# Stick-breaking attention: outputs of two heads side by side, logits of a head in both row halves, fewer abs passes on ScalarE

## The reference, cut to what matters

```python
z = jnp.einsum("bhqd,bhkd->bhqk", qi, kj).astype(jnp.float32)
valid = jnp.logical_or(jnp.logical_not(is_diag), diag_mask)
lo = jnp.where(valid, jax.nn.log_sigmoid(-z), 0.0)
after = jnp.einsum("bhqj,js->bhqs", lo, later) + acc[..., None]
logw = jnp.where(valid, z + lo + after, -jnp.inf)
o = o + jnp.einsum("bhqk,bhkd->bhqd", jnp.exp(logw).astype(vj.dtype), vj).astype(jnp.float32)
acc = acc + jnp.sum(lo, axis=-1)
```

## Time and profile before

| | us |
|---|---|
| median of 3 runs | 2718.43 |
| lowest and highest | 2717.89, 2723.14 |
| the profiled execution's own time | 2719.01 |
| its span, first to last instruction | 2717.3 |
| TensorE busy in it | 2547.8 (94%) |
| GpSimd busy | 1498.4 (55%) |
| VectorE busy | 1039.9 (38%) |
| ScalarE busy | 558.3 (21%) |

### The profile page before, as it was taken

One profiled execution on the slowest core, in us unless ns is written; L12 is line 12 of the kernel. 1 busy time (PEld: TensorE's weight loads), 2 busy tenths in 40 slices (PEclk: granted clock), 3 DMA queues, 4 the chain that ended last, 5 costly groups with the idle time before them and its releaser, 6 DMA issues.

```text
span 2717.3 us, 34707 instructions
## 1 busy us (share of the span) xinstructions
PE 2547.8 (94%) x14410; PEld 2061.8 (76%) x14410; DVE 1039.9 (38%) x1667; ACT 558.3 (21%) x1127; POOL 1498.4 (55%) x1396
## 2 busy tenths in 40 slices
PE   7998997999999998999999989868589998999998
PEld 6778886888888886568888878645488687888887
DVE  3443857163051401336404164973542151421023
ACT  1112323021020113741102021224332210210010
POOL 7444554587496664337749636621121565666664
PEclk9997998999999998999999998989798999999999
DMA  5222022233232231003324313210000222333321
GB/s 165 78 56 63 1 86 85 78 115 95 70 123 94 80 107 62 1 32 105 98 69 124 93 45 90 64 53 16 1 3 2 74 86 85 93 98 97 93 79 69
DMA packets 104289, 199.06 MB, mean 73 GB/s; under 512 B 9306, under 2 KB 12612, under 8 KB 104132
## 3 DMA queue, kind: packets, MB, share of 16 engines
q1 hardware_dynamic: 101476, 189.36, 22.8%
q10 hardware_dynamic: 2656, 7.47, 0.8%
HBM read 194.71 MB, written 2.10 MB: 72 GB/s over the span
## 4 chain that ended last, share of the span: by engine, by line
PE 84%; DVE 10%; ACT 2%; POOL 2%; issue 1%; SPq 0%; DMA 0%; DVEq 0%; POOLq 0%; ACTq 0%
PE psum L153 34%; PE psum L293 23%; PE psum L155 7%; PE psum L232 3%; PE psum L1260 1%; PE psum L1251 1%; PE psum L1279 1%; POOL weight_split_ring L412 1%; DVE big L1810 1%; PE psum L2090 1%; PE psum L2099 1%; DVE best L1809 1%; PE psum L968 1%; PE psum L2075 1%; PE psum L194 1%
## 5 line engine op out<-in xcount | busy, mean ns | idle before, releaser
L412 POOL TENSOR_TENSOR weight_split_ring<-weight_ring,weight_split_ring 128x512 fp32r<-128x512 f32 (+2 forms) x732 | 955.6, 1326 | 30.6
L153 PE MATMUL psum<-x_split,weight_split_ring 128*128 128x512 f32 x4080 | 963.1, 396 | 1.9 <-POOL weight_split_ring L412 1.3
L153 PEld LDWEIGHTS psum<-x_split,weight_split_ring 128*128 128x128 f32 x4080 | 770.2, 190 | 173.3 <-issue 11.8
L409 POOL TENSOR_SCALAR weight_split_ring<-weight_ring 128x1024 fp32r<-128x1024 f32 (+2 forms) x366 | 395.6, 1081 | 759.0 <-PE psum L293 339.9
L293 PE MATMUL psum<-weight_split_ring,hidden_split 128*128 128x512 f32 x2448 | 576.5, 396 | 8.2 <-DVEq L2899 8.2
L293 PEld LDWEIGHTS psum<-weight_split_ring,hidden_split 128*128 128x128 f32 x2448 | 460.3, 188 | 120.0 <-DVEq L2899 8.6
L155 PE MATMUL psum<-weight_split_ring,x_split 128*128 128x512 f32 (+2 forms) x1056 | 238.0, 385 | 2.0 <-DVEq L2899 1.4
L155 PEld LDWEIGHTS psum<-weight_split_ring,x_split 128*128 128x128 f32 x1056 | 195.2, 205 | 43.7 <-issue 7.2
L708 DVE TENSOR_TENSOR big<-big 128x512 f32<-128x512 f32 x64 | 89.0, 1391 | 178.4 <-ACT big L693 178.4
L511 DVE SCALAR_TENSOR_TENSOR residual<-residual,psum 128x512 f32<-128x512 f32 x48 | 32.8, 682 | 261.9 <-PE psum L293 261.9
L693 ACT ACTIVATE big<-psum 128x512 f32<-128x512 f32 x64 | 38.3, 599 | 434.9 <-PE psum L153 378.8
(11 more groups left out here) (329 smaller groups left out, 2627.6 us busy)
## 6 DMA issues: line engine op xcount, KB each, us to landing
weight_ring<-in_mlp_w SPq DMA_DIRECT2D x128, 512.0 KB, 3.8
weight_ring<-in_w_in SPq DMA_DIRECT2D x92, 512.0 KB, 3.6
weight_ring<-in_w_ffn_in SPq DMA_DIRECT2D x40, 512.0 KB, 3.6
weight_ring<-in_w_out SPq DMA_DIRECT2D x24, 512.0 KB, 3.7
weight_ring<-in_w_ffn_out SPq DMA_DIRECT2D x22, 512.0 KB, 3.6
weight_ring<-in_sb_w_q SPq DMA_DIRECT2D x8, 512.0 KB, 3.6
weight_ring<-in_sb_w_k SPq DMA_DIRECT2D x8, 512.0 KB, 3.8
weight_ring<-in_sb_w_v SPq DMA_DIRECT2D x8, 512.0 KB, 3.7
```

What stands on the lines that cost most here:

```text
L153: mm = pe.matmul(out, wp[:, k, m * P:(m + 1) * P], xp, start=first, stop=last)
L409: pool.tensor_scalar(part.high[:, 0:nk, 0:n], raw, 1.0, 0.0, ALU.mult, ALU.add).then_inc(self.high_made, 1)
L412: low = pool.tensor_tensor(part.low[:, k, 0:n], raw[:, k, :], part.high[:, k, 0:n].bitcast(F32), ALU.subtract)
```

## The change

- `out` is done for a pair of heads p (2p, 2p+1) in steps with even h: for each block first the product of the even head, into partitions 0 to 63 of PSUM, then that of the odd head, into 64 to 127 of the same bank. It waits for the selects of both heads. `wt` gets a third buffer. ScalarE's copy and VectorE's `low` handle a pair at once, 128 partitions instead of 64.
- From head 2 on, the logits of blocks 1, 2 and 3 read copies of q and k that stand in the other row half (`m.swap`, two buffers, one a pair); block 0 stays in the head's own half. ScalarE issues the two DMA transfers of a pair's copies: pairs 1 and 2 at the start of the stage, pairs 3 to 7 in steps 4, 6, 8, 10 and 12, behind the weights pass. TensorE waits for them before the first block of a head (`s_sw`).
- For the first two spans (768 columns) softplus is made as Ln(1 + Exp(min(z, 40))) and then the maximum with z. The minimum is a new VectorE pass, `clamp(h)`, PSUM to SBUF; ScalarE does Exp on it, without Abs. Block 0 keeps Abs, Exp(-x), Ln. VectorE's order per step becomes clamp(h+1), softplus(h), low; ScalarE's stays ln(h+1), weights of h, copy.

The diff, cut to its core:

```diff
@@ -1197,9 +1197,9 @@
     s_z = kit.sem("sb_logits_ready")
-    s_abs = kit.sem("sb_abs_ready")
-    s_exp = kit.sem("sb_exp_ready")
-    s_ln = kit.sem("sb_ln_ready")
+    s_sw = [kit.sem(f"sb_other_half_landed{n}") for n in range(2)]
+    s_cl = kit.sem("sb_clamped_logits_ready")
+    s_soft = kit.sem("sb_last_abs_then_exp_then_ln_ready")
     s_lo = kit.sem("sb_softplus_ready")
     s_t = kit.sem("sb_later_blocks_summed")
     s_x = kit.sem("sb_exponent_ready")
@@ -1209,6 +1209,7 @@
     s_oh = kit.sem("sb_out_high_ready")
     s_of = kit.sem("sb_out_read")
+    LINEAR = 40.0
     START = [0, 512, 896, 1152]
     BANK = [(0, 0), (1, 0), (2, 0), (2, 256)]
@@ -1240,6 +1241,16 @@
     def rows(h):
         return slice((h % 2) * 64, (h % 2) * 64 + 64)
+
+    def other_q(h, b):
+        return m.swap[rows(h + 1), (h // 2) % 2, 0, (b - 1) * P:]
+
+    def other_k(h, b):
+        return m.swap[rows(h + 1), (h // 2) % 2, 1, (b - 1) * P:b * P]
+
+    def weights(h, b):
+        c = START[b]
+        return m.wt[:, h % 3, c:c + SEQ - b * P]
     def tensor(pe):
         def logits(h):
@@ -1247,9 +1258,14 @@
                 if h >= 2:
                     pe.wait_ge(s_w, NS * (h - 2) + n + 1)
+                    if n == 0:
+                        pe.wait_ge(s_sw[(h // 2) % 2], 32 * ((h // 2 + 1) // 2))
                 for b in blocks:
-                    mm = pe.matmul(bank(h, b), m.kF[rows(h), h // 2, b * P:(b + 1) * P], m.qF[rows(h), h // 2, b * P:],
-                                   start=(b != 3), stop=True, skip_group_check=True)
+                    if h >= 2 and b >= 1:
+                        k, q = other_k(h, b), other_q(h, b)
+                    else:
+                        k, q = m.kF[rows(h), h // 2, b * P:(b + 1) * P], m.qF[rows(h), h // 2, b * P:]
+                    mm = pe.matmul(bank(h, b), k, q, start=(b != 3), stop=True, skip_group_check=True)
                 mm.then_inc(s_z, 1)
         def exponents(h):
@@ -1269,15 +1285,15 @@
                                        start=False, stop=True, skip_group_check=True)
                 mm.then_inc(s_x, 1)
-        def out(h):
-            if h >= 2:
-
-                pe.wait_ge(s_of, h - 1)
-            o = kit.psum[rows(h), 6 + h % 2, :]
-            pe.wait_ge(s_cut, h + 1)
+        def out(p):
+            if p >= 2:
+
+                pe.wait_ge(s_of, p - 1)
+            pe.wait_ge(s_cut, 2 * p + 2)
             for b in range(NT):
-                mm = pe.matmul(o[:, b * P:], m.vTok[:, b, h * 64:(h + 1) * 64], packed(m.wt, h, b),
-                               start=(b == 0), stop=(b == NT - 1), skip_group_check=True)
+                for h in (2 * p, 2 * p + 1):
+                    mm = pe.matmul(kit.psum[rows(h), 6 + p % 2, b * P:], m.vTok[:, b, h * 64:(h + 1) * 64], weights(h, b),
+                                   start=(b == 0), stop=(b == NT - 1), skip_group_check=True)
             mm.then_inc(s_o, 1)
         logits(0)
@@ -1286,53 +1302,77 @@
                 logits(h + 1)
             if h < SB_HEADS:
                 exponents(h)
-            if h >= 1:
-                out(h - 1)
+            if h >= 2 and h % 2 == 0:
+                out(h // 2 - 1)
     def scalar(act):
         act.preload_act_table_set("natural_log_exp_and_others")
+        def copy_halves(p):
+            if p >= 3:
+
+                act.wait_ge(s_z, NS * (2 * p - 2))
+            for g in range(2):
+                act.dma_start(m.swap[rows(g + 1), p % 2], m.qkF[rows(g), :, p, P:]).then_inc(s_sw[p % 2], 16)
+
         def ln(h):
-            for n, (bk, c, w, _) in enumerate(SPANS):
-                act.wait_ge(s_z, NS * h + n + 1)
-                if h >= 2 and n == 0:
-
-                    act.wait_ge(s_x, NS * (h - 1))
-                ins = act.activation(m.sp[:, h % 2, c:c + w], kit.psum[:, 3 * (h % 2) + bk, 0:w], ACT.Abs)
-            ins.then_inc(s_abs, 1)
-            act.wait_ge(s_abs, h + 1)
-            t = m.sp[:, h % 2, :]
-            act.activation(t, t, ACT.Exp, scale=-1.0).then_inc(s_exp, 1)
-            act.wait_ge(s_exp, h + 1)
-            act.activation(t, t, ACT.Ln, bias=m.one).then_inc(s_ln, 1)
-
+            t, last = m.sp[:, h % 2, :], SPANS[NS - 1][2]
+            act.wait_ge(s_cl, 2 * h + 2)
+            act.activation(t[:, last:], t[:, last:], ACT.Exp)
+            act.wait_ge(s_z, NS * h + NS)
+            if h >= 2:
+
+                act.wait_ge(s_x, NS * (h - 1))
+            act.activation(t[:, 0:last], kit.psum[:, 3 * (h % 2), 0:last], ACT.Abs).then_inc(s_soft, 1)
+            act.wait_ge(s_soft, 3 * h + 1)
+            act.activation(t[:, 0:last], t[:, 0:last], ACT.Exp, scale=-1.0).then_inc(s_soft, 1)
+            act.wait_ge(s_soft, 3 * h + 2)
+            act.activation(t, t, ACT.Ln, bias=m.one).then_inc(s_soft, 1)
+
+        copy_halves(1)
+        copy_halves(2)
         ln(0)
         for h in range(SB_HEADS + 1):
             if h + 1 < SB_HEADS:
                 ln(h + 1)
             if h < SB_HEADS:
-                if h >= 2:
-
-                    act.wait_ge(s_o, h - 1)
+                if h >= 3:
+
+                    act.wait_ge(s_o, (h - 3) // 2 + 1)
                 for n, (bk, c, w, _) in enumerate(SPANS):
                     act.wait_ge(s_x, NS * h + n + 1)
-                    act.activation(m.wt[:, h % 2, c:c + w], kit.psum[:, 3 * (h % 2) + bk, 0:w], ACT.Exp)\
+                    act.activation(m.wt[:, h % 3, c:c + w], kit.psum[:, 3 * (h % 2) + bk, 0:w], ACT.Exp)\
                        .then_inc(s_w, 1)
-            if h >= 1:
-                act.wait_ge(s_o, h)
-                act.activation(m.xin.high[rows(h - 1), (h - 1) // 2, :], kit.psum[rows(h - 1), 6 + (h - 1) % 2, :], ACT.Copy)\
-                   .then_inc(s_oh, 1)
+            if h % 2 == 0 and 4 <= h <= SB_HEADS - 4:
+                copy_halves(h // 2 + 1)
+            if h >= 2 and h % 2 == 0:
+                p = h // 2 - 1
+                act.wait_ge(s_o, p + 1)
+                act.activation(m.xin.high[:, p, :], kit.psum[:, 6 + p % 2, :], ACT.Copy).then_inc(s_oh, 1)
     def vector(dve):
         step = kit.vector_chain(dve)
+        def clamp(h):
+
+            for n, (bk, c, w, _) in enumerate(SPANS[:NS - 1]):
+                dve.wait_ge(s_z, NS * h + n + 1)
+                if h >= 2 and n == 0:
+
+                    dve.wait_ge(s_x, NS * (h - 1))
+                dve.tensor_scalar(m.sp[:, h % 2, c:c + w], kit.psum[:, 3 * (h % 2) + bk, 0:w], LINEAR, None, ALU.min)\
+                   .then_inc(s_cl, 1)
+
         def softplus(h):
-            dve.wait_ge(s_ln, h + 1)
+            dve.wait_ge(s_soft, 3 * h + 3)
             for n, (bk, c, w, _) in enumerate(SPANS):
                 sp = m.sp[:, h % 2, c:c + w]
-                step.mark(dve.scalar_tensor_tensor(out=sp, in0=kit.psum[:, 3 * (h % 2) + bk, 0:w], scalar=0.0, in1=sp,
-                                                   op0=ALU.max, op1=ALU.add))
+                z = kit.psum[:, 3 * (h % 2) + bk, 0:w]
+                if n < NS - 1:
+                    step.mark(dve.tensor_tensor(sp, z, sp, ALU.max))
+                else:
+                    step.mark(dve.scalar_tensor_tensor(out=sp, in0=z, scalar=0.0, in1=sp, op0=ALU.max, op1=ALU.add))
                 if n >= 1:
                     cut(h, n - 1, 1)
             cut(h, NS - 1, 0)
@@ -1343,17 +1383,19 @@
             own = own_queries(m.sp, h, n)
             dve.tensor_tensor(own, own, across(m.upper_strict[:, :], own.shape[1]), ALU.mult).then_inc(s_lo, 1)
-        def low(h):
-            dve.wait_ge(s_oh, h + 1)
-            dve.tensor_tensor(m.xin.low[rows(h), h // 2, :], kit.psum[rows(h), 6 + h % 2, :],
-                              m.xin.high[rows(h), h // 2, :].bitcast(F32), ALU.subtract).then_inc(s_of, 1)
-
-        softplus(0)
+        def low(p):
+            dve.wait_ge(s_oh, p + 1)
+            dve.tensor_tensor(m.xin.low[:, p, :], kit.psum[:, 6 + p % 2, :], m.xin.high[:, p, :].bitcast(F32),
+                              ALU.subtract).then_inc(s_of, 1)
+
+        clamp(0)
         for h in range(SB_HEADS + 1):
             if h + 1 < SB_HEADS:
-                softplus(h + 1)
-            if h >= 1:
-                low(h - 1)
+                clamp(h + 1)
+            if h < SB_HEADS:
+                softplus(h)
+            if h >= 2 and h % 2 == 0:
+                low(h // 2 - 1)
     def gpsimd(pool):
         def sums(h):
@@ -1378,7 +1420,7 @@
             for n in range(NS):
                 pool.wait_ge(s_w, NS * h + n + 1)
                 for b in SPANS[n][3]:
-                    w = packed(m.wt, h, b)[:, 0:P]
+                    w = weights(h, b)[:, 0:P]
                     ins = pool.affine_select(out=w, in_=w, compare_op=ALU.is_gt, fill=0.0, base=0, pattern=[[1, P]],
                                              channel_multiplier=-1)
             ins.then_inc(s_cut, 1)
@@ -2766,10 +2808,12 @@
```

(8 more changed lines are left out.)

## The result

| | before | after |
|---|---|---|
| median of the runs, us | 2718.16 (2714.33 to 2723.14, 4 runs) | 2739.47 (2738.41 to 2742.71, 4 runs) |
| profiled execution | 2719.01 | 2739.0 |
| first logits product of head 2 to that of head 15 | 107.98 | 128.56 |
| first logits product of head 0 to the end of the last subtraction | 141.13 | 165.02 |

The changed kernel is slower, by a ratio of 1.0079 with a 95% interval of 1.0061 to 1.0098. The stage became 23.9 us longer, 20.6 of it between head 2 and head 15. The rest of the profiled execution was 4.0 us shorter, in phases whose instructions are the same: the stage's first product starts at 1054.28 instead of 1058.46, and what follows the stage took 0.2 us more. By the profiles of all twelve kernels here this rest lasts 2568.6 to 2582.9 us, with the same instructions.

A forecast was written before the change was run, and what follows sets the result against it. TensorE alone was taken to bound the attention stage, to be replaced by a serial chain through VectorE. Start -0.6, heads -0.2, end +3.4, copies +4.0, clock +4.2 sum to +10.8 on 2719.0; median 2729, range 2712 to 2742.

The forecast's parts named there:

- start: First chain of the attention stage: only 512 columns of ScalarE's exp remain there, -0.6 us.
- heads, chain alone: Head 2's logits to head 15's: steps of 7.14 and 9.63 us, 107.8 in all against 108.0 before, -0.2.
- copies: Row-half transfers: five exposed, TensorE waits 0.7 to 2.0 us, 1.0 taken, net 0.8 each, +4.0 (ends 0 and +9).
- clock in the heads: TensorE in the stage: three stretches fall to 1.2 GHz at about 1.4 us each, +4.2 (ends 0 and +20).
- end: After head 15's logits: its softplus stands behind the low subtraction of heads 12 and 13, +3.4 us together.
- The bound and its loss: Attention stage: TensorE alone bounds it; its 28 us saving is eaten by the serial chain logits, clamp, softplus, exponents.
- ScalarE's lighter work: ScalarE in the heads: two abs passes (0.49 us each) and half a copy fewer, worth nothing except -0.6 at the start.
- the clock falls in most heads: Rival, TensorE's clock in the stage: 12 stretches fall, 17 us instead of 4, 2742 and more; chance 0.11.
- Chain only: Rival, attention stage: copies land in time and the clock holds, +2.6, 2721 us (2716 to 2724); chance 0.23.
- Column halves don't overlap: Rival, outputs of two heads: the column halves don't run side by side, +2.3 us a pair, +18, near 2747; chance 0.02.

The follow-up runs named there:

- A: The changed kernel without the row-half copies, logits of every block in the head's own row half: 2722.83 us, ratio 1.0027 to the kernel before.
- D: The changed kernel with row-half copies issued one pair earlier and seven needless products in each wait for VectorE: 2727.32 us, ratio 1.0032 to the kernel before.
- C: The changed kernel with seven needless TensorE products in each wait for VectorE, copies issued as in the change: 2732.0 us, ratio 1.0054 to the kernel before.
- H: The kernel before with only the outputs of two heads side by side, softplus, VectorE's order and logits as before: 2702.76 us, ratio 0.9942 to it.
- E: The changed kernel with VectorE's order alone changed, softplus(h+1) right behind clamp(h+1): 2706.0 us, ratio 0.9959 to the kernel before.
- B: The changed kernel with the copies of pairs 3 to 7 issued two heads sooner, nothing else: 2730.26 us, ratio 1.0053 to the kernel before.
- I: The kernel before with only the clamp softplus and the new VectorE and ScalarE orders, outputs head by head: 2756.35 us, ratio 1.0122 to it.

## Why the prediction was right, and where its sum was not

The time lay in the range and on the side that was forecast, but the slowdown was twice the predicted one. That it stayed in the range was luck in part: the stage became 23.9 us longer, which on 2718.4 gives 2742.3, just above the upper end of 2742; the 4.0 us that brought it back lie in phases that the change leaves alone. By the terms of the sum, for the profiled executions:

| term | predicted | measured | from |
|---|---|---|---|
| start | -0.6 | -2.0 | first logits of head 0 to those of head 2: 15.91, now 13.88 |
| heads, chain alone | -0.2 | +1.3 | A and D: 109.2 and 109.3, before 107.98 |
| copies | +4.0 | +6.8 | C without its fallen stretch, 116.1, less D's 109.3 |
| clock in the heads | +4.2 | +12.5 | 128.56 less 116.1 |
| end | +3.4 | +5.3 | head 15's logits to the last subtraction: 17.24, now 22.58 |
| outside the stage | 0 | -4.0 | same instructions, other clock |
| sum | +10.8 | +19.9 | spans 2717.3 and 2737.2 |

**The bound and its loss: right.** TensorE alone set the time before, as H shows, and the order on VectorE put one serial chain in its place. Its links were those of the prediction, from the start of the logits: clamp at 0.92 (0.95 predicted), softplus at 2.04 (2.07), exponents at 3.44 to 3.48 (3.48). TensorE stood still 1.6 to 2.0 us (1.9). E shows that it was the order and not the work: the same passes in another order are 33 us faster.

**The heads: mis-sized by 1.5.** Predicted steps were 7.14 and 9.63, measured 7.45 and 9.55. The delay of 0.20 by the subtraction came one step later than it was counted, and only there (exponents 3.68 after the logits). The exponents took 3.77 instead of 3.66, most likely since the later cuts now come only as TensorE wants them; the prediction named that price, 0.1 a head for each tenth, and set it to nothing.

**The copies: mis-sized by 2.8.** The wait was 1.54 each (five, 7.7 in all), inside the 0.7 to 2.0 that the rows gave, but not the 1.0 that was taken. The second copy landed 3.8 us after the outputs' start, where the prediction had 3.0 to 4.3 and took 3.3: 3.0 us from its issue, more than the 2.5 that the earlier trace rows has for 256 KB, and the issue itself only 0.75 after the outputs' start instead of 0.5. A step with the wait is 11.16 us instead of 9.55, 1.61 more. The next step gets 0.25 of it back (7.2 instead of 7.45), since the subtraction is then out of the way of the clamps: 1.36, five times.

**The clock: the mechanism right, the count wrong.** A fallen stretch costs 1.5 to 1.7 us in B and 1.3 in I, predicted 1.4. But there were nine of them between head 2 and 15 instead of three, and one more in the last exponents. C shows the cause: keep TensorE running in the chain's waits and all but one of the fallen stretches go, with the copies' waits as they were (7.7 us). B tells what raised the count, by one profile of each: with the chain's waits alone four stretches fell, with the copies' waits added, nine. The rival in which the clock falls in most heads (12 stretches, 17 us) was nearer in this term than the forecast was. The Trainium skill (TensorE: Matmul & The Clock Gate, A second HAM failure mode: psum-queue depth-cycling) describes such a fall through many short stops in place of one long one; the trace agrees, with stops of 1.5 to 2.0 us.

**The end: right but for the clock.** The last exponents start 12.31 after the last logits (12.17 predicted). From there to the last outputs it took 6.54 us, predicted 4.73; a stretch at 1.2 GHz lies in it, which makes up most of the 1.9 that the term is off (in E, at full clock, the same part took 4.98).

**ScalarE's lighter work: worth nothing in the heads, as said.** At the start the gain was 2.0 us and not 0.6, but one stretch of 3.4 us at 1.2 GHz fewer (three instead of four) is in it. H, with ScalarE's passes there as before and also three such stretches, took 13.51 us from head 0 to head 2, where the changed kernel took 13.88 and the kernel before 15.91. So no run shows a gain from the lighter work.

**The rivals.** "Chain only" was the right figure for A (2722.83, predicted 2721 with 2716 to 2724): it is what the change costs without copies and their part of the clock. "Column halves don't overlap" is refuted by 2.38 us a pair.

## What to carry to other kernels

Before an engine that is the bound gets less work, look at what its new waits would hang on: a pass put at the front of another engine's order (here clamp(h+1) ahead of softplus(h)) can turn a head's slack into one serial chain, and moving one call gives it back. A transfer that is issued in the step that needs it costs what that step doesn't cover of its landing (here 3.0 us to land, 1.36 lost each time), and waits of 1.6 to 2.0 us in each step of 7 to 11 can cost TensorE's clock on top (12.5 us in the changed kernel, 6.3 in B against D, nothing in the second half of B). Both are priced from the number of steps, not as a rarity. Try the parts alone: the simplest one, outputs side by side, was worth 15 us by itself.

## What was not expected of the hardware

- The same waits did and did not bring the clock down: in B four times in the first half of the stage, never in the second.
- Runs of one kernel can lie in groups: A had 2718.2 to 2718.5 at a mean clock of 0.966 and 2729.9 to 2730.6 at 0.960, I had 2738.7 and 2757.8. It is tempting to blame the chain's waits. A's profile, of the upper group, shows the clock at 1.00 from head 2 to head 15, so at least A's groups come from outside these heads.
- Needless products cost less than standing still: seven products of 128 columns, 1.83 us in each head, made the stage 11.2 us shorter.
- Two copies of 192 KB between SBUF addresses held ScalarE's DMA queue for 1.26 us and landed 3.0 us after their issue.
- Products in different row halves start out of program order. The program has block 0 last, and the timeline shows its first instruction (1126.51, 64x512 from `big`) ahead of three of the other half (1126.61 and 1127.05, from `gain_rows`). The Trainium skill (TensorE: Matmul & The Clock Gate, The mechanism) says that products start and end in program order; the recorded starts differ from it by 0.1 to 0.5 us. The ends are modelled, so no row here bears on them.
